# Two stacked layers with an RWKV-7 mixer on one core: value tokens centred while they are turned, key features made a step earlier, norm squares added before their sum

## The reference

```python
def rmsnorm(x, g):
    r = lax.rsqrt(jnp.mean(x * x, axis=-1, keepdims=True) + EPS)
    return (x * r) * g

# first layer, between the mixer and the FFN
h = h + merged @ w_o[l]
u2 = rmsnorm(h, g_ffn[l])

# RWKV mixer: 32 heads of 64
kk = kk / jnp.maximum(jnp.linalg.norm(kk, axis=-1, keepdims=True), 1e-12)
k = k * (1 + (a - 1) * k_a)
y = _wkv7_scan(r, decay, k, v, -kk, kk * a)      # state S, per head 64 x 64
mean = jnp.mean(y, axis=-1, keepdims=True)
var = jnp.mean(jnp.square(y - mean), axis=-1, keepdims=True)
y = ((y - mean) * lax.rsqrt(var + GN_EPS_2)).reshape(B, L, D_INNER)
y = y * ln_w + ln_b
bonus = (jnp.sum(r * k * r_k, axis=-1, keepdims=True) * v).reshape(B, L, D_INNER)
y = (y + bonus) * jax.nn.silu(g)
m = y @ w_out
h = h + _rms_norm(m, norm_post[i])
```

## Time and profile before

| | us |
|---|---|
| median of 3 runs | 1518.45 (1517.3 to 1520.14) |
| the profiled execution | 1518.34 |
| its span in the trace | 1516.5 |
| TensorE matmul busy | 1465.6 |
| VectorE busy | 1022.5 |
| ScalarE busy | 889.0 |

### The profile page before, as it was taken

How to read it: one execution, slowest core, us unless ns; L and a number is a source line. 1 busy time by engine, 2 the same in 40 slices (tenths; PEclk the granted TensorE clock), 3 DMA queues, 4 the chain that set the end, 5 groups by cost and what they waited for, 6 DMA issues and landing times.

```text
span 1516.5 us, 27310 instructions
## 1 busy us (share of the span) xinstructions
PE 1465.6 (97%) x10692; PEld 1319.4 (87%) x10692; DVE 1022.5 (67%) x1931; ACT 889.0 (59%) x2102; POOL 58.1 (4%) x30
## 2 busy tenths in 40 slices
PE   7999999999999999898999999999999999999997
PEld 7899777887999999797889898888989888799986
DVE  3468386547678875787677777777777545667764
ACT  4456444664557775466666666666666545555653
POOL 1444000000000000000000000000000000000000
PEclk9999999999999999999999999999999999999999
DMA  9555234121555555242011111111011135333340
GB/s 375 175 187 169 92 112 166 57 72 68 176 181 185 181 179 185 82 139 84 29 57 56 57 32 54 57 57 56 29 57 56 45 116 216 115 113 135 113 135 33
DMA packets 27183, 169.94 MB, mean 112 GB/s; under 512 B 3744, under 2 KB 6192, under 8 KB 7472
## 3 DMA queue, kind: packets, MB, share of 16 engines
q1 hardware_dynamic: 25872, 167.09, 31.6%
q10 hardware_dynamic: 1184, 1.11, 0.3%
HBM read 167.12 MB, written 1.06 MB: 111 GB/s over the span
## 4 chain that ended last, share of the span: by engine, by line
PE 87%; ACT 8%; DVE 3%; issue 1%; DMA 1%; DVEq 0%; SPq 0%; ACTq 0%
PE bank L785 10%; PE bank L786 10%; PE bank L787 10%; PE bank L1118 3%; PE bank L873 3%; PE bank L1302 3%; PE bank L927 3%; PE bank L1286 3%; PE bank L769 2%; PE bank L1120 2%; PE bank L1119 2%; PE bank L1138 2%; PE bank L1279 1%; PE bank L820 1%; PE bank L1213 1%
## 5 line engine op out<-in xcount | busy, mean ns | idle before, releaser
L685 DVE TENSOR_TENSOR ring_lo<-ring,w_hi_rw 128x1024 fp32r<-128x1024 f32 x126 | 153.6, 1221 | 49.6 <-ACT w_hi_rw L1566 48.7
L685 DVE TENSOR_TENSOR w_lo<-ring,w_hi 128x1024 fp32r<-128x1024 f32 x84 | 103.3, 1232 | 78.9 <-ACT w_hi L1566 78.3
L1566 ACT ACTIVATE w_hi_rw<-ring 128x1024 fp32r<-128x1024 f32 x126 | 132.4, 1053 | 38.6 <-PE bank L1483 15.7
L1118 PE MATMUL bank<-x_hi,w_hi_rw 128*128 128x272 f32 x384 | 133.9, 349 | 1.1 <-ACT arena L1534 0.3
L1566 ACT ACTIVATE w_hi<-ring 128x1024 fp32r<-128x1024 f32 x106 | 111.8, 1057 | 28.5 <-PE bank L787 15.0
L1534 ACT ACTIVATE arena<-bank 128x272 f32<-128x272 f32 (+2 forms) x165 | 67.2, 408 | 90.2 <-PE bank L787 51.9
L1120 PE MATMUL bank<-x_hi,ring_lo 128*128 128x272 f32 x384 | 111.3, 290 | 0.0
L1119 PE MATMUL bank<-x_lo,w_hi_rw 128*128 128x272 f32 x384 | 111.0, 289 | 0.0
L785 PE MATMUL bank<-u_hi,w_hi 128*128 128x256 f32 x320 | 90.8, 284 | 1.4 <-DVE w_lo L685 1.4
L787 PE MATMUL bank<-u_hi,w_lo 128*128 128x256 f32 x320 | 90.6, 283 | 0.0
L786 PE MATMUL bank<-u_lo,w_hi 128*128 128x256 f32 x320 | 90.5, 283 | 0.0
(11 more groups left out here) (514 smaller groups left out, 4499.5 us busy)
## 6 DMA issues: line engine op xcount, KB each, us to landing
ring<-wstream SPq DMA_DIRECT2D x151, 1024.0 KB, 4.9
con<-consts SPq DMA_DIRECT2D x1, 2400.0 KB, 15.0
h<-xT SPq DMA_DIRECT2D x1, 1024.0 KB, 6.0
sq<-spread SPq DMA_DIRECT2D x1, 1024.0 KB, 5.1
arena<-wlora ACTq DMA_DIRECT2D x1, 1024.0 KB, 5.1
out<-arena SPq DMA_DIRECT2D x4, 256.0 KB, 2.6
arena<-decays SPq DMA_DIRECT2D x2, 384.0 KB, 5.7
arena<-spread SPq DMA_DIRECT2D x1, 768.0 KB, 6.6
```

The lines of the kernel that those rows point to most:

```text
L685: ops.tensor_tensor(lo, whole, hi.bitcast(F32), ALU.subtract).then_inc(S(signal), 1)
L1118: nc.tensor.matmul(b[:, 0:T2], w_hi, x_hi[:, x, k, :], start=k == 0, stop=False)
L1566: nc.scalar.activation(hi, whole, ACT.Copy).then_inc(S("w_hi_ready"), 1)
```

## The change

The centring matrix takes the place of the identity for the value tokens, so that `y` comes out centred; the centring matmul of `y` and its semaphore go, and ScalarE copies and squares `y` straight from bank 7 in `take_ys`. The scaling reads `ys` instead of bank 5, and TensorE waits for `rw_sd` (bank 6 read) instead of `rw_normed`. `feats_last` moves ahead of the wait for level 6's product. The bonus matmul waits for the step after which `tk` is written (`rw_step` of level 5 of the pair before) instead of `rw_feats`, and the second gram group waits for level 6's result, which reads bank 4. In two norms VectorE adds squares 1 to 6 onto square 0 (`add_squares`), and TensorE sums two tiles instead of eight (`sum_ends`).

```diff
@@ -820,6 +820,15 @@
                 ins = nc.tensor.matmul(bank[2][:, 0:T], C("ones"), sq[:, slot + t, 0:T], start=t == 0, stop=t == nt - 1)
                 if t == nt - 1:
                     ins.then_inc(S("norm_sum"), 1)
+            def sum_ends(n, T):
+                pe.wait_ge(S("squares_added"), n)
+                nc.tensor.matmul(bank[2][:, 0:T], C("ones"), sq[:, 0, 0:T], start=True, stop=False)
+                squares[0] += DT
+                pe.wait_ge(S("norm_sq"), squares[0])
+                nc.tensor.matmul(bank[2][:, 0:T], C("ones"), sq[:, DT - 1, 0:T], start=False, stop=True).then_inc(S("norm_sum"), 1)
 
             def norm(nt, T, slot=0):
                 for t in range(nt):
@@ -1034,13 +1043,10 @@
                 project_split(dn_hi, dn_lo, DT)
             for m in range(DT):
                 project_split(mg_hi, mg_lo, DT, None if m else "mix_lo_ready", 4)
-                if m >= 2:
-                    sum_tile(m - 2, DT, T1)
             b = free_bank()
             for k in range(DT):
                 if k == DT - 2:
-                    sum_tile(DT - 2, DT, T1)
-                    sum_tile(DT - 1, DT, T1)
+                    sum_ends(1, T1)
                 pe.wait_ge(S("hg_ready"), DT + k + 1)
                 ins = nc.tensor.matmul(b[:, 0:T1], weights(), hg[:, k, :], start=k == 0, stop=k == DT - 1)
             ins.then_inc(S("proj_done"), 1)
@@ -1101,7 +1107,10 @@
                         if j == R_KK:
                             pe.wait_ge(S("rw_kk2"), q + 1)
                         if j == R_BONUS:
-                            pe.wait_ge(S("rw_feats"), q + 1)
+                            if q == 0:
+                                pe.wait_ge(S("rw_feats"), 1)
+                            else:
+                                pe.wait_ge(S("rw_step"), 7 * q - 1)
                         current[0] = free_bank()
                     b = current[0]
                     if j in (R_W, R_A):
@@ -1178,8 +1187,9 @@
 
             def to_tokens(p, c, b):
                 t0, n = RCH[c]
-                for j, src in enumerate((gin[:, p % 2, 4, :], bk[:, 1, :], bk[:, 0, :])):
-                    ins = nc.tensor.transpose(bank[b][0:n, j * P:(j + 1) * P], src[:, t0:t0 + n], C("ident"))
+                nc.tensor.matmul(bank[b][0:n, 0:P], gin[:, p % 2, 4, t0:t0 + n], C("center64"), start=True, stop=True)
+                for j in range(2):
+                    ins = nc.tensor.transpose(bank[b][0:n, (j + 1) * P:(j + 2) * P], bk[:, 1 - j, t0:t0 + n], C("ident"))
                 ins.then_inc(S("rw_toks"), 1)
 
 
@@ -1227,10 +1237,6 @@
                     ins = nc.tensor.matmul(bank[7][f, t], tok[0:n, p % 2, c, 0, f], gram_of(p, c, j, 3), start=False, stop=True)
                 ins.then_inc(S("rw_yc"), 1)
 
-            def center(p):
-                pe.wait_ge(S("rw_ys"), p + 1)
-                nc.tensor.matmul(bank[5][:, 0:T2], C("center64"), ys, start=True, stop=True).then_inc(S("rw_centered"), 1)
-
             def variance(p):
                 pe.wait_ge(S("rw_sq"), p + 1)
                 nc.tensor.matmul(bank[6][:, 0:T2], C("mean64"), sqr, start=True, stop=True).then_inc(S("rw_var"), 1)
@@ -1246,13 +1252,15 @@
                 pe.wait_ge(S("rw_feats"), p + 1)
                 grams(p, 1)
                 fill(fill_end(p, "low_rank"))
+                if p >= 1:
+                    pe.wait_ge(S("rw_step"), 7 * p)
                 grams(p, 2)
                 fill(fill_end(p, "grams"))
                 if p == PAIRS - 1:
                     assert pn[0] % 2 == 1
                     fill_out(4)
                 if p >= 2:
-                    pe.wait_ge(S("rw_normed"), p - 1)
+                    pe.wait_ge(S("rw_sd"), p - 1)
                 grams(p, 0)
                 turned_grams(p)
                 fill(fill_end(p, "gram0"))
@@ -1308,12 +1316,10 @@
                     fill(fill_end(p, f"delta{l}"))
                     if p == PAIRS - 1:
                         fill_out(2)
-                if p >= 1:
-                    center(p - 1)
             pe.wait_ge(S("rw_step"), 7 * PAIRS)
             variance(PAIRS - 2)
             fill_out(10)
-            pe.wait_ge(S("rw_normed"), PAIRS - 1)
+            pe.wait_ge(S("rw_sd"), PAIRS - 1)
             for c in range(3):
                 chain_z(PAIRS - 1, c)
                 fill_out(2)
@@ -1321,21 +1327,15 @@
                 fill_out(2)
                 chain_y(PAIRS - 1, c)
                 fill_out(2)
-            center(PAIRS - 1)
             fill_out(3)
             variance(PAIRS - 1)
             fill_out(16)
             pe.wait_ge(S("rw_pair_done"), PAIRS)
             fill_out(5 + IT)
             pe.wait_ge(S("proj_taken"), pn[0] + 1)
-            for i in range(4):
-                sum_tile(i, DT, T2)
             fill_out(IT)
-            for i in range(4, 6):
-                sum_tile(i, DT, T2)
             fill_out(IT)
-            for i in range(6, 8):
-                sum_tile(i, DT, T2)
+            sum_ends(2, T2)
             assert outs_filled[0] == 8 * IT
             pn[0] += 8
 
@@ -1978,14 +1978,10 @@
             def take_ys(p):
                 act.wait_ge(S("rw_yc"), 3 * p + 3)
                 if p >= 1:
-                    act.wait_ge(S("rw_centered"), p)
+                    act.wait_ge(S("rw_normed"), p)
+                    act.wait_ge(S("rw_var"), p)
                 nc.scalar.activation(ys, bank[7][:, 0:T2], ACT.Copy).then_inc(S("rw_ys"), 1)
-
-            def square(p):
-                act.wait_ge(S("rw_centered"), p + 1)
-                if p >= 1:
-                    act.wait_ge(S("rw_var"), p)
-                nc.scalar.activation(sqr, bank[5][:, 0:T2], ACT.Square).then_inc(S("rw_sq"), 1)
+                nc.scalar.activation(sqr, bank[7][:, 0:T2], ACT.Square).then_inc(S("rw_sq"), 1)
 
             def deviation(p):
                 act.wait_ge(S("rw_var"), p + 1)
@@ -2030,8 +2026,6 @@
             take_until(RW_AHEAD)
             split_rw(1, R_R)
             for p in range(PAIRS):
-                if p >= 2:
-                    square(p - 2)
                 take_until(fill_end(p, "start"))
                 if p >= 2:
                     deviation(p - 2)
@@ -2090,7 +2084,6 @@
                         round_yo(4 * l - 4, min(4 * l, PAIRS - 2))
                 if p >= 1:
                     take_ys(p - 1)
-            square(PAIRS - 2)
             deviation(PAIRS - 2)
             for c in range(3):
                 chain_z(PAIRS - 1, c)
@@ -2099,7 +2092,6 @@
                     round_yo(PAIRS - 2, PAIRS - 1)
                 split_hi(rw_end + c + 1)
             take_ys(PAIRS - 1)
-            square(PAIRS - 1)
             deviation(PAIRS - 1)
             split_hi(rw_end + 5)
             round_yo(PAIRS - 1, PAIRS)
@@ -2512,12 +2504,24 @@
                 dve.wait_ge(S("mix_hi_ready"), 4 + b + 1)
                 V_.tensor_tensor(mg_lo[:, b, :], gr[:, b, :], mg_hi[:, b, :].bitcast(F32), ALU.subtract).then_inc(S("mix_lo_ready"), 1)
 
+            def add_squares(b, base, T):
+                dve.wait_ge(S("norm_sq"), base + b + 1)
+                ins = V_.tensor_tensor(sq[:, 0, 0:T], sq[:, 0, 0:T], sq[:, b, 0:T], ALU.add)
+                if b == DT - 2:
+                    ins.then_inc(S("squares_added"), 1)
+                else:
+                    link(ins)
             def add_to_h(outs, first, base):
 
                 for b in range(DT):
                     split_both(down_units(b) if base else min(first_units + 6 + b + HALVES, mix_end))
                     dve.wait_ge(S("proj_taken"), first + b + 1)
                     V_.tensor_tensor(h[:, b, META:], h[:, b, META:], outs[:, b, :], ALU.add).then_inc(S("h_tile"), 1)
+                    if not base and 2 <= b:
+                        add_squares(b - 1, DT, T1)
                     if base and 1 <= b < DT - 1:
                         dve.wait_ge(S("norm_sq"), 2 * DT + 2 * b + 2)
                         link(V_.tensor_tensor(sq[:, 0, 0:T1], sq[:, 0, 0:T1], sq[:, b, 0:T1], ALU.add))
@@ -2682,7 +2686,8 @@
 
                 dve.wait_ge(S("rw_sd"), p + 1)
                 link(V_.reciprocal(sdn, sdn))
-                V_.scalar_tensor_tensor(out=sdn, in0=bank[5][:, 0:T2], scalar=V("rwkv_ln_w_2", p), in1=sdn, op0=ALU.mult, op1=ALU.mult)\
+                dve.wait_ge(S("rw_ys"), p + 1)
+                V_.scalar_tensor_tensor(out=sdn, in0=ys, scalar=V("rwkv_ln_w_2", p), in1=sdn, op0=ALU.mult, op1=ALU.mult)\
                     .then_inc(S("rw_normed"), 1)
 
             def finish(p):
@@ -2834,6 +2839,7 @@
                         feats_norm(p + 1, 0)
                     elif ahead and l == 6:
                         feats_unit(p + 1)
+                        feats_last(p + 1)
                     dve.wait_ge(S("rw_delta"), 6 * p + l)
                     if l < 4:
                         odd, delta = U0p[l % 2][0:META, 1], bank[4][0:META, 2 * P:2 * P + META].rearrange("p (g n) -> p g n", g=2)
@@ -2860,9 +2866,7 @@
```

(6 more changed lines are left out.)

## The result

The kernel after takes 1502.7 us, median of 4 executions (1501.11 to 1504.37), against 1518.59 for the kernel before on the same chip: a ratio of 0.9895, 95% interval 0.9878 to 0.9912. It is 15.9 us faster; forecast were 11.8 us and 1506.5, range 1502.0 to 1512.0. The profiled execution took 1504.37 us (span 1502.6), which is 13.97 less than that of before. One execution further down (of both edits together) ran at a mean clock of 0.75 and took 1797 us; none of its rows is used.

What follows compares the result with a forecast made beforehand. TensorE, in flight for 97% of the span, was taken to bound the kernel. Pairs 4.8, tail with RWKV norm sums 4.4 and mixer 2.6 make 11.8 us off the profiled 1518.34: 1506.5, range 1502.0 to 1512.0.

Steps and rivals of the forecast that it cites:

- part 1: Norm squares added on VectorE: six sums go in each of two projections, saving 2.6 us (mixer) and 2.75 us (RWKV output).
- The tail: Behind the pairs: variance 1.2 us earlier, last centring 0.46 saved; with norm sums of 2.75, 4.4 us.
- The pair: Each of pairs 2 to 14: centring matmul's 0.46 saved less 0.11 for tokens, net 0.35 us, 4.5 over 13.
- the last call: Third token call of a pair, behind the token-copy wait: its f32 matmul replacing a transpose costs 0.11 us, paid in full.
- The boundary: Between pairs on TensorE: the variance starts at 919.97 instead of 920.70, 0.73 us earlier, without waiting for the square.
- keep their distances: Bonus matmul and first gram stay as far behind the variance as before, so move by 0.73 us if features are there.
- The mask: VectorE's mask at 927.75 moves 0.46 us earlier, limited by VectorE being free at 927.29.
- Pairs 1 and 15: First and last pairs with partial gains: 0.3 us saved in pair 1, 0.1 in pair 15.
- (a): Rival: ScalarE's chain does not hold the tokens; a pair gives 0.62, 3.5 us more in 13 pairs, 1503.0; chance 0.16.
- (b): Rival: a wait takes back all the pairs gain; 7.0 us is left, 1511.3; chance 0.16.
- (c): Rival: f32 matmul among token transposes costs 0.44, another 10.6 us, 1517.1, no change; chance 0.04.
- (d): Rival: level's result, behind three VectorE operations, holds the second gram group; slower, 1528.2; chance 0.02.

Runs made afterwards that it cites:

- both edits together: Kernel after with the centring matmul last in each token call and VectorE's reciprocal and scaling of y later: 1502.33 us, median of three.
- Experiment 1: Kernel before with only the added norm squares (add_squares, sum_ends): 1511.57 us, ratio 0.9952.
- experiment 3: Kernel before with only the move of the last key features and the two changed waits: 1517.95 us, ratio 0.9993.
- the eighth experiment: Kernel after, unchanged, measured a second time: 1502.11 us, ratio 0.9896.
- Experiment 6: Kernel after with VectorE's reciprocal and scaling of y moved behind the gram masks, finish to level 2: 1502.2 us, ratio 0.99.
- experiment 2: Kernel after with the last key features and the bonus matmul's wait put back: 1513.27 us, ratio 0.9966.
- experiment 4: Kernel after with value tokens turned by a plain transpose, centring of y left out: 1500.81 us, ratio 0.988.

## Why the prediction was right, and where it was off

**Right in kind.** TensorE bounds the kernel, what goes from it is saved, and the three stages gave what was named. Experiment 1 shows part 1 by itself: 2.4 and 2.8 for 2.6 and 2.75; TensorE waits for none of VectorE's additions. The tail gave 0.5 for the last centring (0.46) and 1.2 for the wait and the centring ahead of it (1.2).

**The pair.** It gave 0.47, forecast was 0.35. The forecast's ledger was 0.46 for what ScalarE's chain lets through, less 0.11 for the last call. Four of its figures were off:
- The boundary gave 0.73 as forecast, and 0.11 more: "keep their distances" was wrong. A variance matmul that has waited takes 0.57 until the next, one that has not takes 0.45 (experiment 3). This does not reach the end of the pair; it adds to the slack ahead of the tokens.
- The mask came 0.58 earlier, not 0.46 (0.73 at the variance, less 0.15: it stands 7.05 behind the variance before and 7.20 after). I let VectorE start the mask at the end of the operation before it (927.56), but it starts each operation some 0.08 before the last record ends (923.84 to 924.45 is 0.61 for a record of 0.69). ScalarE closed up by 0.09 more on the way to its token copy (9.55 behind the variance, then 9.61), which was so 0.67 earlier.
- So the wait before the last call fell from 0.29 to 0.22; I had it grow to 0.34. "TensorE's idle time for the token copy at least as large as the 5.2 us of before" was wrong: 3.7.
- The last call takes 0.22 more than before, not 0.11, for the pause, which the rows that I priced it from (128 columns) do not show. 0.67 - 0.22 = 0.45 is the sum, within 0.02 of the period.

**Pairs 1 and 15.** Pair 15 loses 0.2, where I had 0.1 saved: its tokens cost 0.58 more than before, with the same pause in the last call and no later wait that hides the first two. Pair 1 gives 0.2 from its tokens on, where I had 0.3; pair 0 cannot be told from the half-clock stretches near it (695 and 726 before, 698 after).

**The rest is the clock, and there the time was lucky.** 12.9 us between the two profiles belong to the change, with pair 1 it is 13.1, or 1.3 more than forecast. By that alone the median would be 1505.5 (an estimate, 1518.59 less 13.1). What the medians have beyond it, 2.8 us, is of the size of what the twelve matmuls at 1255 gain by running at full clock, and it brings the median to within 0.7 of the low end of the range. The prediction has no clock in it. Whose gain this is stays open: both traces of the kernel after (the eighth experiment is the second) have no half-clock stretch behind that norm, and the traces of the kernel before and of all eight other experiments that left a usable one do, of 3.4 or 6.8 us, though the matmuls behind that norm are the same code in all of them. That may be chance, or it may hang on where in time the kernel after reaches the norm.

**The rivals.** (a) asked for the chain not to hold the tokens at all; TensorE still waits 0.22 for it and a pair gives 0.47 and not 0.62, so it fell, though its time of 1503.0 is close: it is near by the clock and not by its mechanism. Experiment 6 shows that VectorE's chain is the holder. (b), all of the pairs' gain given back, did not come; experiment 2 shows where it lives: without the feature move the pairs lose 0.1 each, and the gain of 13 x 0.57 is the move's, in this kernel. That the two parts are worth 0 (experiment 3) and -0.1 (experiment 2) a pair alone and 0.47 together is the reading of the whole change. (c) fell: 0.22 for an f32 matmul of 128 columns against 0.11 for a transpose, in the earlier trace rows and in the tokens after. The Trainium skill (TensorE: Matmul & The Clock Gate, Terms) has the transpose mode four times faster for FP32; between an f32 transpose and an f32 matmul of 128 columns these traces show two. The Trainium skill's page Perfetto Trace Analysis (Transposes) prefers a transpose to a standard matmul for a logical transpose; experiment 4 prices what ignoring it costs here, 0.2 us a pair, against 0.46 for the centring matmul that it saves. (d), TensorE waiting for the level's result, did not appear: VectorE ended it at 917.97, and the second gram group starts later.

## What to carry to other kernels

When a matmul ahead of a stage goes, ask for every operand of the next ones, not only for the one that was waited for: here the square and the last features were 0.6 us apart, and only both together gave anything. A constant matrix can ride on a transpose for the difference between an f32 matmul and a transpose, and where a wait follows, part of that is hidden. Before believing a gain of 2 or 3 us between two profiles of 1500, list the half-clock stretches of both; the usual period of a regular loop, read in stretches at full clock, settles 0.1 us.

## What was not expected of the hardware

- Stretches of 3.4 or 6.8 us at 1.2 GHz come and go between executions of one and the same kernel (at 182 us: there in after, absent in its repetition), and TensorE loses up to half their length: 3.4 of 6.8 us at 182, 2.8 of 6.8 at 1266.
- In the token calls there is a pause of 0.1 us on each side of an f32 matmul with a 16-column stationary (0.55 for the call with one inside, 0.64 with two, 0.33 for three plain transposes), and none with 128 columns.
- The variance matmul (f32, 272 columns) holds the next matmul 0.11 us longer when it had to wait than when it had not (0.57 and 0.45). The centring matmul of the first token call of pair 15, the one call of 128 columns that waits, holds the next 0.29 (1177.28 to 1177.57) instead of 0.22. What causes it no run here shows.
